# Two-layer float32 trunk on one core: 128 bytes put between the activation parts and the weight rings

## The reference

```python
def swiglu_ffn(h, w_gate_up, w_down):
    gate, up = jnp.split(h @ w_gate_up, 2, axis=-1)
    return (jax.nn.silu(gate) * up) @ w_down

def reference(x, ...):
    h = x                                     # (1, 256, 2048)
    # layer 0: stick-breaking attention, w_qkv 2048 x 6144, w_o 2048 x 2048
    h = h + stick_breaking_mixer(rmsnorm(h, sb_norm[0]), sb_w_qkv[0], sb_w_o[0])
    h = h + swiglu_ffn(rmsnorm(h, ffn_norm[0]), ffn_w_gate_up[0], ffn_w_down[0])
    # layer 1: chunked gMLP, w_in 2048 x 4096, w_o 2048 x 2048
    h = h + chunked_gmlp_mixer(rmsnorm(h, gm_norm[0]), gm_w_in[0], gm_v_norm[0], gm_w_s[0], gm_b_s[0], gm_w_o[0])
    h = h + swiglu_ffn(rmsnorm(h, ffn_norm[1]), ffn_w_gate_up[1], ffn_w_down[1])
    return rmsnorm(h, final_norm)
```

## Time and profile before

| what | value |
|---|---|
| median of 2 runs | 2072.2 us (2070.47 to 2073.94) |
| profiled execution, its own time | 2069.99 us |
| its span, first to last instruction | 2068.3 us |
| TensorE busy | 2058.8 us of it, 9279 matmuls |
| granted TensorE clock | 0.999 of full speed |
| VectorE, ScalarE busy | 1430.0 us, 1011.4 us |
| DMA | 402.47 MB, mean 195 GB/s |

### The profile page before, as it was taken

How to read it: one execution, slowest core, us unless ns; L and a number is a source line. 1 busy time by engine, 2 the same in 40 slices (tenths; PEclk the granted TensorE clock), 3 DMA queues, 4 the chain that set the end, 5 groups by cost and what they waited for, 6 DMA issues and landing times.

```text
span 2068.3 us, 27155 instructions
## 1 busy us (share of the span) xinstructions
PE 2058.8 (100%) x9279; PEld 1721.7 (83%) x9279; DVE 1430.0 (69%) x1822; ACT 1011.4 (49%) x1285; POOL 16.4 (1%) x30
## 2 busy tenths in 40 slices
PE   9999999999999999999999999999999999999998
PEld 7888888888888888888888888888888888888887
DVE  7787787867766677666557887877766677665454
ACT  6677765544444444444445444554444444444443
POOL 1000000000000000000000000000000000000000
PEclk9999999999999999999999999999999999999999
DMA  8555655666666666556567665566666666655554
GB/s 276 183 188 158 188 187 172 199 198 195 195 191 200 195 197 195 195 194 201 195 196 211 193 203 186 191 194 204 195 191 202 194 198 196 191 198 201 194 194 152
DMA packets 207419, 402.47 MB, mean 195 GB/s; under 512 B 12336, under 2 KB 13056, under 8 KB 206976
## 3 DMA queue, kind: packets, MB, share of 16 engines
q1 hardware_dynamic: 206496, 398.11, 61.8%
q0 software_dynamic: 688, 3.18, 0.4%
q10 hardware_dynamic: 176, 0.40, 0.1%
HBM read 399.55 MB, written 2.10 MB: 194 GB/s over the span
## 4 chain that ended last, share of the span: by engine, by line
PE 99%; issue 0%; ACT 0%; DVE 0%; POOLq 0%; POOL 0%; DVEq 0%; ACTq 0%
PE acc L1101 65%; PE acc L1109 32%; PE tp L1205 1%; PE tp L1185 1%; PE tp L1334 0%; PE acc L1151 0%; PE tp L1117 0%; PE acc L1144 0%; PE acc L1377 0%; PE acc L1375 0%; PE acc L1376 0%; ACT xT L382 0%; PE tp L1193 0%; DVE h L1070 0%; ACT junk L640 0%
## 5 line engine op out<-in xcount | busy, mean ns | idle before, releaser
L672 DVE TENSOR_TENSOR w_lo<-raw,w_hi 128x1024 fp32r<-128x1024 f32 x750 | 915.7, 1224 | 560.5 <-ACT w_hi L364 558.6
L364 ACT ACTIVATE w_hi<-raw 128x1024 fp32r<-128x1024 f32 x750 | 791.7, 1059 | 894.7 <-PE acc L1109 889.9
L1101 PE MATMUL acc<-w_hi,xT 128*128 128x512 f32 x4080 | 996.9, 385 | 0.0
L1101 PEld LDWEIGHTS acc<-w_hi,xT 128*128 128x128 f32 x4080 | 762.6, 187 | 148.2
L1109 PE MATMUL acc<-w_lo,xT 128*128 128x512 f32 x2040 | 539.0, 385 | 0.0
L1109 PEld LDWEIGHTS acc<-w_lo,xT 128*128 128x128 f32 x2040 | 381.9, 187 | 74.1
L1101 PE MATMUL acc<-w_hi,hid_lo 128*128 128x512 f32 x944 | 364.4, 386 | 0.0
L1101 PE MATMUL acc<-w_hi,hid_hi 128*128 128x512 f32 x944 | 362.3, 384 | 0.0
L1109 PE MATMUL acc<-w_lo,hid_hi 128*128 128x512 f32 x944 | 249.5, 385 | 0.0
L1101 PEld LDWEIGHTS acc<-w_hi,hid_lo 128*128 128x128 f32 x944 | 176.9, 187 | 36.4
L1109 PEld LDWEIGHTS acc<-w_lo,hid_hi 128*128 128x128 f32 x944 | 176.7, 187 | 34.4
(11 more groups left out here) (117 smaller groups left out, 428.3 us busy)
## 6 DMA issues: line engine op xcount, KB each, us to landing
raw<-in_ffn_w_gate_up SPq DMA_DIRECT2D x352, 512.0 KB, 4.5
raw<-in_ffn_w_down SPq DMA_DIRECT2D x176, 512.0 KB, 3.7
raw<-in_sb_w_qkv SPq DMA_DIRECT2D x95, 512.0 KB, 4.3
raw<-in_gm_w_in SPq DMA_DIRECT2D x64, 512.0 KB, 4.5
raw<-in_sb_w_o SPq DMA_DIRECT2D x32, 512.0 KB, 4.2
raw<-in_gm_w_o SPq DMA_DIRECT2D x32, 512.0 KB, 4.1
h<-in_x SPq DMA_DIRECT2D x3, 512.0 KB, 8.8
gain_bc<-in_gm_v_norm POOLq DMA_DIRECT2D x1, 1024.0 KB, 6.2
```

What stands on the lines that cost most here:

```text
L364: nc.scalar.activation(w_hi[:, p % RING], raw[:, p % RING], ACT.Copy).then_inc(hi_ready, 1)
L672: nc.vector.tensor_tensor(w_lo[:, p % RING], raw[:, p % RING], w_hi[:, p % RING].bitcast(f32), ALU.subtract).then_inc(lo_ready, 1)
L1101: nc.tensor.matmul(swept(acc_at(chunk, r)), part[:, kt, rs], swept(w_hi[:, p % RING, k]), start=(kt == 0 and part is hi), stop=False)
```

## The change

A filler tensor `skew` of 128 bytes per partition is allocated between `xT` and `raw`. The three rings and all that stands behind them up to `lead_in` move by 128 bytes. `lead_in` is computed so that `region` keeps its old remainder: it shrinks from 160 bytes to 32, and `region` stays at its old address. After it the remainder of the rings modulo 512 is 128 more than that of `xT`, `hid_hi` and `hid_lo`. The three rings keep their places relative to one another. No instruction is added, removed or moved on any engine, and no wait changes; only addresses do.

```diff
         xT = sb("xT", [P, KD, 2, S], f32r)
         xT_hi, xT_lo = xT[:, :, 0], xT[:, :, 1]
+        SKEW = 128
+        skew = sb("skew", [P, SKEW // 4])
         raw = sb("raw", [P, RING, KP, CH])
...
-        lead_in = sb("lead_in", [P, (nc.lookup_mloc(w_hi).addr - used_up_to) % CH // 4])
+        lead_in = sb("lead_in", [P, (nc.lookup_mloc(w_hi).addr - SKEW - used_up_to) % CH // 4])
         region = sb("region", [P, 2 * KF * S])
         R0 = nc.lookup_mloc(region).addr
-        assert (R0 - nc.lookup_mloc(w_hi).addr) % CH == 0
+        assert (R0 + SKEW - nc.lookup_mloc(w_hi).addr) % CH == 0
```

## The result

2122.29 us median (2122.19 to 2122.39) against 2072.2: the ratio is 1.0242, 95% interval 1.0198 to 1.0286. The kernel became slower by 50 us; that it is slower is clear, that it is so by 2% or more is not quite, since the interval begins just under that. The forecast was 2072, the range 2035 to 2135; the time lies inside the range, but in the case that I had given 0.22. The profiled execution of the changed kernel has a span of 2120.5 us, at the same granted clock of 0.999.

The account below looks back on a forecast made before the run. TensorE's 9024 large matmuls, one behind the other, were taken to bound the kernel. The profiled 2069.99 us plus 0 for the change, with the median 2.2 us above that execution, gave 2072 us; range 2035 to 2135.

Parts of the forecast that it names:

- What bounds the kernel: TensorE: 9024 large matmuls one behind the other at 223.4 ns, 2016 us, plus 52 us of the rest; no waits.
- lever of 9.0 us per nanosecond: All large matmuls on TensorE: one nanosecond more or less on each is 9.0 us, 0.44% of the time.
- Nothing of 512 bytes and above counts: TensorE's two operand reads: address distances in multiples of 512 leave the mean matmul duration at 385 ns.
- If 16-byte places within 64 bytes are what collides, a shift of 128 changes nothing ... I take 0.: TensorE's moving against stationary read: 128 is a multiple of 64, so the shift costs 0 us; chance of no change 0.50.
- bounds of -54 and +126 us: All large matmuls as short as the shortest (-6 ns each) or as long as the longest (+14 ns each).
- hint of 13.3 ns: Matmul starts: excess per group of four or seven is 3 or 7 times 13.3 ns, one 64-byte group of the load.
- 213.3 ns of the prediction: One large matmul on TensorE: 512 columns at 2.4 GHz, leaving 10.1 ns of each 223.4 as excess.
- The splits, the DMAs, what moves along: nothing.: ScalarE's and VectorE's splits, writes into `raw`, small tensors: no cost on the path; small tensors under 1 us either way.
- more collisions: Every large matmul: address bits 64 to 256 count, equal starts are good; +7 ns each, +63 us, 2135 us; chance 0.22.
- a slower rhythm: Long stretches keep the slower known rhythm, 2.720 instead of 2.681 us per piece: +30 us, 2102 us; chance 0.10.
- rule of two independent read ports: TensorE's SBUF reads: loading the next stationary tile takes no bandwidth from the running matmul, so no shift matters; not taken as settled.

Follow-up runs that it names:

- all plain: Every large matmul in plain column order, none swept, with the rings at distance 0 and at 128: 2096.85 and 2147.84 us.
- all swept: Kernel before and changed kernel without the plain matmul of every fourth piece, so every large matmul is swept: 2095.13 us at distance 0, 2110.78 at 128.
- one ring alone: Against the kernel before, only `w_hi` moved by 128 bytes, with `raw`, `w_lo` and all others left in place modulo 512: 2125.14 us.
- three placed knocks: Changed kernel with distance 64 and plain matmuls only at gate-up piece 3 of both layers and piece 7 of layer 1: 2044.39 us.

## Why the prediction was wrong

*What bounds the kernel* held. The time is the cadence of the 9024 large matmuls, and nothing waits: all 52 us of the loss are in TensorE's busy time, idle time before a matmul stays 0.0. The lever of 9.0 us per nanosecond was right (6.2 ns gave 50 us, the attention stretch less than its share).

*"Nothing of 512 bytes and above counts"* held where it was tried (the rings 512 bytes further, 2069.96 us); nothing of 256 does either, as 256 against 0 and 320 against 64 show.

*"If 16-byte places within 64 bytes are what collides, a shift of 128 changes nothing ... I take 0."* This is the step that failed. In place of the 0 the distance of 128 put 6.2 ns on each matmul, 52 us of TensorE's busy time. I had bounds of -54 and +126 us from the rows, and chose 0 between them by reading a cause out of the order of the sweeps. Distance 64 (-8 us), 128 (+50 us) and 192 (+28 us) are all multiples of 64 and all different. And the sweeps are not its cause: all plain, the distance of 128 costs 51 us (all swept it costs 16, so the order acts on the size). The hint of 13.3 ns was weak, too. The grouping itself was right (218 230 224 221 in the steady rhythm; 234 239 225 226 220 222 221, seven, in the slower one), but the unit was not: at distance 64 the excess over the 213.3 ns of the prediction is 6.7 ns per matmul in the rhythm 220, at all-plain order 13.3 each, at 128 66.7 ns for four and 26.7 for each of the 240s. 6.7 ns divides them all, 13.3 does not divide the first. That the time still lies in the range comes from the wide bounds, not from the reading.

*The splits, the DMAs, what moves along: nothing.* Held: the run that moved `raw` and the small tensors took 2069.96 us, and in the profile after the splits have 1224 and 1060 ns as before.

*The rival "more collisions"* had the place and the size: every large matmul, a mean of 390 to 391 ns where I had written 392, 2122 us for 2135. That the size was so near is luck, since 392 was just half way to the longest. Its mechanism was a story and is not confirmed. It spoke of reads that meet more often, in each matmul by itself; the matmuls on an unmoved ring got slower too (one ring alone), shorter loads did not help at distance 0, and at one distance of 128 there are rhythms of 240, 229.9 and 225.1 ns.

*The rival "a slower rhythm"* was the right kind of thing, and I had its evidence before me, two rhythms at one alignment in the earlier trace rows. I used it only to price a switch between the two that I knew. The distance does not choose between known rhythms; it makes other ones. The Trainium skill's rule of two independent read ports ("TensorE: Matmul & The Clock Gate", section "Step-by-step: what each phase is for") disagrees with the runs, and they decide: the address of one of TensorE's operands against the other moves the time by -8 to +50 us with the same instructions. So in their effect the two reads are not independent of each other here; at which place in the chip they meet, no run shows.

What stays open is how a rhythm comes about: which access of the one read holds up which of the other, and what carries the state from one matmul to the next. No run separates a load's read from the moving read beside it, since in nearly all the starts both begin within 4 ns of each other. Nor was a kernel tried that sets the 220 rhythm anew behind each block of attention's small matmuls, which end it at 89 us and disturb it in all of that stage.

## What to carry to other kernels

Where TensorE streams float32r matmuls without a gap, the spacing of starts is worth listing to the nanosecond: a repeating pattern there may hold a reserve that no wait shows. Here the excess over the prediction's 213.3 ns came to 91 us, of which these runs won back 26; the shortest rhythm seen was 220. Try the distance between the stationary and the moving operand at a few values under 256 bytes, each with a full run, since neither the sign nor the size could be worked out from the trace of another distance. Then look at what throws the pattern out (an odd matmul, an inserted block), because one knock in the right phase can be worth more than the distance: the distance of 64 alone gave 8 us, with three placed knocks 26.

## What the runs showed that I had not expected

- The relative address of the two operands decides which cadences a kernel can fall into, and of this distance only what is left modulo 256 bytes counted in the pairs tried: 223.4 ns at 0 and 256, 229.6 at 128, 220.0 to 223.3 at 64, with not one instruction changed. Without the plain matmuls it is 226.5 at 0 and 240, 229.9 and 225.1 at 128.
- Rhythms sustain themselves over hundreds of microseconds and have memory: 222 225 and 220 220 run under the same instructions at distance 64, and which one holds depends on where one plain matmul fell, hundreds of matmuls earlier.
- The plain matmul in every fourth piece is no mere cost: taking these away, each some 5.5 ns longer than its neighbours at distances 0 and 128, made the kernel 25 us slower at 0 and 12 us faster at 128.
- A stationary load of 32 columns for 128 takes 107 ns for 187, and the matmuls beside it get no shorter.
